# One VectorE instruction that adds the bias, scales and folds the maximum in every attention

## The reference, cut to what matters

```python
# sliding window of the first block: a mask, and a sink as one more column
s = jnp.einsum('bnqhgd,bnkhd->bnhgqk', qb, kk).astype(jnp.float32) * (D ** -0.5)
s = jnp.where(valid[None, :, None, None], s, -1e30)
p = jax.nn.softmax(jnp.concatenate([s, sink], axis=-1), axis=-1)[..., :-1]
# differential attention of the second block: a bias by distance, two softmaxes
s = jnp.einsum('bqmhd,bkmhd->bmhqk', qi, k).astype(jnp.float32) * (Dk ** -0.5) + bias
s = jnp.where(dist >= 0, s, -jnp.inf)
p = jax.nn.softmax(s, axis=-1)
w = p[:, 0] - lam * p[:, 1]
o = jnp.einsum('bhqk,bkhd->bqhd', w.astype(v.dtype), v)
# latent attention of the odd layer: a causal mask only
s = (jnp.einsum('bqhd,bkhd->bhqk', qn, k_nope) + jnp.einsum('bqhr,bkr->bhqk', qr, k_rope)) * scale
s = jnp.where((start + jnp.arange(Q_BLOCK))[:, None] >= kpos[None, :], s, -jnp.inf)
p = jax.nn.softmax(s, axis=-1).astype(v.dtype)
```

## Time and profile before

| | |
|---|---|
| three runs | 2165.37, 2166.03, 2175.59 us; median 2166.03 |
| profiled execution | span 2161.3 us from the first to the last instruction (no time of its own beside it; the median is 4.7 us above this span) |
| TensorE busy | 2005.7 us (93%), 9889 matmuls |
| VectorE busy | 1158.1 us (54%), 1710 instructions |
| ScalarE busy | 964.1 us (45%), 1758 instructions |
| mean granted TensorE clock | 0.970 |

### The profile page before, as it was taken

One profiled execution on the slowest core, in us unless ns is written; L12 is line 12 of the kernel. 1 busy time (PEld: TensorE's weight loads), 2 busy tenths in 40 slices (PEclk: granted clock), 3 DMA queues, 4 the chain that ended last, 5 costly groups with the idle time before them and its releaser, 6 DMA issues.

```text
span 2161.3 us, 25017 instructions
## 1 busy us (share of the span) xinstructions
PE 2005.7 (93%) x9889; PEld 1489.3 (69%) x9889; DVE 1158.1 (54%) x1710; ACT 964.1 (45%) x1758; POOL 12.7 (1%) x28
## 2 busy tenths in 40 slices
PE   8999889999889998779999999999888899999997
PEld 4875455776456887446788888787555578888885
DVE  6624955623965223946655543532676676555433
ACT  4735755734664332554422222344566644222223
POOL 2000000000000000000000000000000000000000
PEclk8999989999899999899999999999999999999999
DMA  8331342231212532003233333333400023333331
GB/s 296 109 86 54 142 117 59 82 86 49 79 39 68 166 98 59 1 1 112 69 98 98 98 91 98 95 100 82 132 1 1 21 88 88 98 98 98 88 100 47
DMA packets 301265, 183.11 MB, mean 85 GB/s; under 512 B 17550, under 2 KB 292108, under 8 KB 299948
## 3 DMA queue, kind: packets, MB, share of 16 engines
q1 hardware_dynamic: 295437, 166.05, 26.5%
q10 hardware_dynamic: 4704, 13.31, 1.7%
q0 software_dynamic: 1008, 2.15, 0.3%
HBM read 179.22 MB, written 2.27 MB: 84 GB/s over the span
## 4 chain that ended last, share of the span: by engine, by line
PE 78%; DVE 14%; ACT 5%; issue 2%; DMA 1%; DVEq 0%; ACTq 0%
PE PS L901 22%; PE PS L903 21%; PE PS L902 21%; PE PS L1057 2%; PE PS L1044 2%; PE PS L1072 2%; DVE SE L2145 2%; DVE TINY L2161 1%; DVE WLO L2075 1%; PE PS L1013 1%; DVE X L2042 1%; DVE S L2223 1%; ACT WHI L1510 1%; ACT SE L1638 1%; DVE SE L2192 1%
## 5 line engine op out<-in xcount | busy, mean ns | idle before, releaser
L902 PE MATMUL PS<-LO,WHI 128*128 128x512 f32 x1690 | 660.0, 391 | 0.0
L901 PE MATMUL PS<-HI,WHI 128*128 128x512 f32 x1578 | 627.0, 397 | 24.8 <-DVE LO L2048 10.0
L903 PE MATMUL PS<-HI,WLO 128*128 128x512 f32 x1578 | 616.4, 391 | 0.0
L2075 DVE TENSOR_TENSOR WLO<-RING,WHI 128x1024 fp32r<-128x1024 f32 (+3 forms) x271 | 314.5, 1161 | 530.5 <-ACT WHI L1510 529.4
L1510 ACT ACTIVATE WHI<-RING 128x1024 fp32r<-128x1024 f32 (+3 forms) x271 | 272.6, 1007 | 468.9 <-PE PS L903 446.5
L901 PEld LDWEIGHTS PS<-HI,WHI 128*128 128x128 f32 x1578 | 297.3, 188 | 107.9 <-issue 26.6
L902 PEld LDWEIGHTS PS<-LO,WHI 128*128 128x128 f32 x1690 | 318.9, 189 | 65.0 <-issue 1.7
L903 PEld LDWEIGHTS PS<-HI,WLO 128*128 128x128 f32 x1578 | 297.3, 188 | 63.4
L901 PE MATMUL PS<-HIDDEN,WHI 128*128 128x512 f32 x352 | 137.1, 390 | 0.6 <-PE PS L903 0.6
L903 PE MATMUL PS<-HIDDEN,WLO 128*128 128x512 f32 x352 | 137.0, 389 | 0.0
L902 PE MATMUL PS<-HIDDEN,WHI 128*128 128x512 f32 x352 | 136.9, 389 | 0.0
(11 more groups left out here) (342 smaller groups left out, 2361.1 us busy)
## 6 DMA issues: line engine op xcount, KB each, us to landing
RING<-in_ffn_w_up SPq DMA_DIRECT2D x88, 512.0 KB, 3.8
RING<-in_w_in SPq DMA_DIRECT2D x48, 512.0 KB, 3.8
RING<-in_w_mod SPq DMA_DIRECT2D x32, 512.0 KB, 4.4
RING<-in_ffn_w_down SPq DMA_DIRECT2D x32, 512.0 KB, 4.0
RING<-in_ev_w_in SPq DMA_DIRECT2D x30, 512.0 KB, 3.8
RING<-in_w_out SPq DMA_DIRECT2D x16, 512.0 KB, 4.3
RING<-in_od_w_in SPq DMA_DIRECT2D x15, 512.0 KB, 3.9
RING<-in_ffn_w_down SPq DMA_DIRECT2D x16, 384.0 KB, 3.4
```

The costliest lines, as they stand in the source:

```text
L901: mm(bank, WHI[i2][:, i, :], hi, start=(k == 0), stop=False)
L902: mm(bank, WHI[i2][:, i, :], lo, start=False, stop=False)
L903: return mm(bank, WLO[i2][:, i, :], hi, start=False, stop=last)
L2075: tt(WLO[i2][:, 0:nk, :], raw, WHI[i2][:, 0:nk, :], ALU.subtract).then_inc(me.signals(w_split), 1)
```

## The change

VectorE's two passes over the scores become one instruction for each head and group, `tensor_tensor_reduce`. It computes out = (score + bias) x (-scale) and folds min(first, out) over the row into one value per query, which it writes beside the output. So scores are kept negated, the minimum is the negated maximum, and ScalarE's exponential takes scale -1 instead of 1. For this the table of biases is multiplied by eight where it is evicted (the scale of these attentions is 1/8; masks are 0 or -1e30 and need nothing), and the sinks are negated once, at the start of the first mixer stage. The first value of the minimum is 3e38, in the sliding window the negated sink, and in the later groups of a joint unit the minimum of the group before, for which VectorE waits. In the sliding window the copy of the sinks goes ahead of the wait for the scores.

The semaphores `at_free` and `at_max` become one, `at_scaled`, counted once for each new instruction; `swa_free` and `swa_max` become `swa_scaled`. ScalarE waits before each exponential for the instruction that made its input. TensorE waits for both instructions of a group before it writes into the group's banks again, and in the sliding window for the one of the same bank.

```diff
                 def scores(u, g):
                     if g["free"]:
-                        pe.wait_ge(at_free, g["free"])
+                        pe.wait_ge(at_scaled, g["free"])
...
                 def scores(i):
                     u = todo[i]
-                    if n0 + i:
-                        pe.wait_ge(swa_free, n0 + i)
                     for a in range(2):
+                        if n0 + i:
+                            pe.wait_ge(swa_scaled, 2 * (n0 + i) - 1 + a)
...
                 def exp(u, i):
-                    if i == 0:
-                        act.wait_ge(at_max, u["maxima"])
+                    act.wait_ge(at_scaled, u["maxima"][i])
...
-                    fn(x, x, ACT.Exp, bias=UNIT_MAX[u["n"] % 2][:, at:at + 1], scale=1.0,
+                    fn(x, x, ACT.Exp, bias=UNIT_MAX[u["n"] % 2][:, at:at + 1], scale=-1.0,
...
                     n = todo[i]["n"] + 1
-                    act.wait_ge(swa_max, n0 + i + 1)
                     for a in range(2):
                         at = 2 * (i % 3) + a
-                        fn(pair_e(i % 3, a, n), PAIR_S[:, i % 3, a, 0:n], ACT.Exp, bias=NMAX[:, at:at + 1], scale=1.0,
+                        act.wait_ge(swa_scaled, 2 * (n0 + i) + a + 1)
+                        fn(pair_e(i % 3, a, n), PAIR_S[:, i % 3, a, 0:n], ACT.Exp, bias=NMAX[:, at:at + 1], scale=-1.0,
...
-                        fn(VECS_SB[:, c:c + w], bank[0:16, 0:w], ACT.Copy).then_inc(me.signals(acc_free_act), 1)
+                        fn(VECS_SB[:, c:c + w], bank[0:16, 0:w], ACT.Copy, scale=8.0).then_inc(me.signals(acc_free_act), 1)
...
-                    for g in u["groups"]:
+                    for n, g in enumerate(u["groups"]):
                         dve.wait_ge(at_scores, g["ready"])
-                        both = PS[:, g["bank"]:g["bank"] + 2, 0:g["n"]]
-                        if u["gates"] and g["side"]:
-                            both = PS[:, g["bank"], 0:2 * g["n"]].rearrange("p (a n) -> p a n", a=2)
-                        stt(buf[:, :, g["c"]:g["c"] + g["n"]], both, u["scale"], g["bias"],
-                            ALU.mult, ALU.add).then_inc(me.signals(at_free), 1)
-                    dve.wait_ge(*me.last)
-                    if u["joint"]:
-                        nc.vector.tensor_reduce(nmax[:, 0:2], buf, AX.X, ALU.max, negate=True).then_inc(me.signals(at_max), 1)
-                        return
...
+                        for a in range(2):
+                            at = u["softmaxes"][a if u["joint"] else 2 * n + a][3]
+                            score = PS[:, g["bank"] + a, 0:g["n"]]
+                            if u["gates"] and g["side"]:
+                                score = PS[:, g["bank"], a * g["n"]:(a + 1) * g["n"]]
+                            first = HUGE
+                            if u["joint"] and n:
+                                dve.wait_ge(at_scaled, g["count"] - 3 + a)
+                                first = nmax[:, at:at + 1]
+                            nc.vector.tensor_tensor_reduce(buf[:, a, g["c"]:g["c"] + g["n"]], score, g["bias"][:, a, :], -u["scale"],
+                                                           first, ALU.add, ALU.min, nmax[:, at:at + 1]).then_inc(at_scaled, 1)
...
-                    dve.wait_ge(swa_scores, 2 * (n0 + i + 1))
-                    stt(PAIR_S[:, r, :, 0:n], PS[:, 0:2, 0:n], 64 ** -0.5, u["bias"].unsqueeze(1).broadcast_to([P, 2, n]),
-                        ALU.mult, ALU.add).then_inc(me.signals(swa_free), 1)
                     nc.vector.tensor_copy(PAIR_S[:, r, :, n:n + 1], SINKS[:, h0:h0 + 2].unsqueeze(2)) \
                         .then_inc(me.signals(dve_step), 1)
-                    dve.wait_ge(*me.last)
-                    nc.vector.tensor_reduce(NMAX[:, 2 * r:2 * r + 2], PAIR_S[:, r, :, 0:n + 1], AX.X, ALU.max, negate=True) \
-                        .then_inc(me.signals(swa_max), 1)
+                    for a in range(2):
+                        dve.wait_ge(swa_scores, 2 * (n0 + i) + a + 1)
+                        nc.vector.tensor_tensor_reduce(PAIR_S[:, r, a, 0:n], PS[:, a, 0:n], u["bias"], -64 ** -0.5,
+                                                       SINKS[:, h0 + a:h0 + a + 1], ALU.add, ALU.min,
+                                                       NMAX[:, 2 * r + a:2 * r + a + 1]).then_inc(swa_scaled, 1)
...
+                        ts(SINKS, SINKS, -1.0, None, ALU.mult).then_inc(me.signals(dve_step), 1)
+                        dve.wait_ge(*me.last)
                     mixers(l)
```

More of the change, by code:

```diff
@@ L32 @@
 NEG = -1e30
+HUGE = 3e38
 LAYERS = 2
@@ L317, in build @@
         acc_ready, acc_free_act, acc_free_dve = sem("acc_ready"), sem("acc_free_act"), sem("acc_free_dve")
-        at_scores, at_free, at_max, at_exp, at_probs, at_turned, at_turn_free, at_values, at_mixed = (
-            sem(f"at_{n}") for n in ("scores", "free", "max", "exp", "probs", "turned", "turn_free", "values", "mixed"))
+        at_scores, at_scaled, at_exp, at_probs, at_turned, at_turn_free, at_values, at_mixed = (
+            sem(f"at_{n}") for n in ("scores", "scaled", "exp", "probs", "turned", "turn_free", "values", "mixed"))
         sq_ready, sq_used, rstd_ready, normed = sem("sq_ready"), sem("sq_used"), sem("rstd_ready"), sem("normed")
@@ L330, in build @@
         keys_to_exp, keys_exp, keys_ready = (sem(n) for n in ("keys_to_exp", "keys_exp", "keys_ready"))
-        swa_scores, swa_free, swa_max, swa_exp, swa_recip, swa_probs, swa_turned, swa_turn_free, swa_values, swa_mixed = (
-            sem(f"swa_{n}") for n in ("scores", "free", "max", "exp", "recip", "probs", "turned", "turn_free", "values", "mixed"))
+        swa_scores, swa_scaled, swa_exp, swa_recip, swa_probs, swa_turned, swa_turn_free, swa_values, swa_mixed = (
+            sem(f"swa_{n}") for n in ("scores", "scaled", "exp", "recip", "probs", "turned", "turn_free", "values", "mixed"))
         ret_scores, ret_masked, ret_values, ret_mixed = (sem(f"ret_{n}") for n in ("scores", "masked", "values", "mixed"))
@@ L667, in count_units @@
         def count_units():
-            n_unit = n_score = n_free = n_max = n_exp = n_prob = n_value = 0
+            n_unit = n_score = n_scaled = n_exp = n_prob = n_value = 0
             mains, sides = [], []
@@ L676, in count_units @@
                     g["bank"] = 4 if g["side"] else 2 * (len(mains) % 2)
-                    n_score, n_free = n_score + 2, n_free + 1
-                    g["ready"], g["count"] = n_score, n_free
-                    seen.append(n_free)
-                n_max += u["side"] + 1 if not u["joint"] else 1
+                    n_score, n_scaled = n_score + 2, n_scaled + 2
+                    g["ready"], g["count"] = n_score, n_scaled
+                    seen.append(n_scaled)
                 n_exp += len(u["softmaxes"])
@@ L683, in count_units @@
                 n_value += 2
-                u["maxima"], u["exps"], u["probs"], u["done"] = n_max, n_exp, n_prob, n_value
+                u["exps"], u["probs"], u["done"] = n_exp, n_prob, n_value
+                u["maxima"] = [n_scaled - 1 + a for a in range(2)] if u["joint"] else \
+                    [g["count"] - 1 + a for g in u["groups"] for a in range(2)]
                 u["turn"], u["ring"] = len(TURN_BANK), len(OWNER)
@@ L1076, in head_sums @@
                 def head_sums():
-                    pe.wait_ge(at_free, units[-1]["groups"][-1]["count"])
+                    pe.wait_ge(at_scaled, units[-1]["groups"][-1]["count"])
                     for k in range(4):
@@ L2147, in scaled @@
-                    dve.wait_ge(*me.last)
-                    if u["joint"]:
-                        nc.vector.tensor_reduce(nmax[:, 0:2], buf, AX.X, ALU.max, negate=True).then_inc(me.signals(at_max), 1)
-                        return
-                    c, k, m = 0, 0, u["n_main"]
-                    if u["side"]:
-                        c, k = u["groups"][0]["n"], 2
-                        nc.vector.tensor_reduce(nmax[:, 0:2], buf[:, :, 0:c], AX.X, ALU.max, negate=True) \
-                            .then_inc(me.signals(at_max), 1)
```

8 lines of the change are left out of this document (removed).

## The result

The changed kernel takes 2134.82 us (median of 4 runs, 2131.75 to 2140.63) against 2168.28 us for the kernel before, measured beside it: a ratio of 0.9855, 95% interval 0.9837 to 0.9872. The profiled execution has a span of 2131.7 us, its own time is 2133.54 us. In every profiled execution on record the time is 1.8 to 2.0 us above the span; so of the 4.7 us that the prediction carried over, some 2.8 were a profiled execution that was quicker than its median. From span to span the gain is 29.6 us.

The account below looks back on a forecast made before the run. TensorE holds 78% of the chain, but VectorE's passes hold it up in five attention stretches. Savings of 5 + 8 + 7 + 3 = 23 us take the span from 2161.3 to 2138.3; with 4.7 carried over, 2143 us, range 2132 to 2163.

Parts of the forecast that it names:

- the 4.7 us that the prediction carried over: Whole kernel: the median of the runs, 2166.03 us, lay this far above the profiled span and was added to the forecast.
- The 23 us: All attention stages: forecast gain in span, summed from 5 for mixers, 8 even, 7 gated and 3 causal.
- rival (c): New VectorE instruction everywhere: streams at half rate, 2.08 ns an element, so the kernel ends slower, 2182 us; chance 0.12.
- rival (a): New VectorE instructions, 122 on the chain: the accumulator costs its full 0.19 us, leaving 2156 us; chance 0.18.
- Mixer, 5 us: Sliding window pairs in both mixer layers: 0.38 us saved a full pair, 0.13 a half; 5.7 us on the chain, 5 kept.
- Even attention, 8 us: First part of the even attention: differential and first two joint units save 11.3 us on the chain, 8 kept.
- Gated units, 7 us: Odd attention's gated units: 1.8 us saved for 512 elements and 1.2 for 384; 8.4 us on the chain, 7 kept.
- the full 8.4: Odd attention's gated units: saving in us if every piece on the chain counts, four of 1.8 and one of 1.2.
- the lower end of the range: Whole kernel: 2132 us, from the full 29.5 us of savings and some clock that denser work gives back.
- Causal units, 3 us: Odd attention's causal units: passes save 5.2 us, but TensorE waited only 4.1 us for VectorE, so 3 kept.
- the cap of 4.1: Odd attention's causal units: TensorE waited only this many us for VectorE, so no more could be gained.
- Rival (b): Even, gated and causal stretches: TensorE becomes the bound, its waits turning to ScalarE or its own order; 2154 us; chance 0.14.

Follow-up runs that it names:

- swa_only: Changed kernel with the new instruction only in the sliding window of both mixer stages, all other attention put back to the two passes; ratio 0.9983 to the kernel before.
- even_only: Changed kernel with the new instruction only in the even attention's differential and joint units, the rest put back to the two passes; ratio 0.9962 to the kernel before.
- causal_only: Changed kernel with the new instruction only in the odd attention's causal units, the rest put back to the two passes; ratio 0.9994 to the kernel before.
- after_again: The changed kernel as it is, profiled and timed a second time; median 2136.33 us, ratio 0.9859 to the kernel before.
- gated_only: Changed kernel with the new instruction only in the odd attention's 16 gated units, the rest put back to the two passes; ratio 0.9929 to the kernel before.
- coarse_waits: Changed kernel, but ScalarE waits once a unit for all new instructions instead of before each exponential; 2140.31 us, ratio 0.9871 to the kernel before.
- after_filled: Changed kernel with unread matmuls ahead of TensorE's probability waits in joint units, differential units and both mixer stages; 2141.39 us, ratio 0.988 to the kernel before.
- the filled kernels: Kernels with unread matmuls ahead of TensorE's probability waits: the kernel before at ratios 1.0015 and 1.001, the changed one at 0.988, with an added reduction 0.9919.
- dose_three: Changed kernel with three extra VectorE reductions of 256 constant elements in each gated unit; 2152.01 us, ratio 0.9927 to the kernel before.
- dose_one_filled: Changed kernel with one extra VectorE reduction and three or one unread matmuls ahead of TensorE's probability wait in each gated unit; 2147.78 us, ratio 0.9919.

## Why the prediction was right, and where its size was off

The mechanism that was forecast is there: TensorE's waits for VectorE shrank where the chain of work had shown them. The 23 us are close to the 21.5 us by which TensorE's idle time fell, but the parts of the sum miss in both directions: the mixers gave nearly nothing and the even part's waits too little, the gated and causal units more than was kept. That they nearly cancel is luck. The other part of the gain is the clock, which the sum didn't hold.

**All gated-stage profiles together.** Old code (before, swa_only, even_only, causal_only): 107.1 to 111.0 us, idle 21.7 to 23.5, clock 0.83 to 0.89. New code (after, after_again, gated_only, coarse_waits, after_filled): 88.3 to 94.0 us, idle 14.1 to 14.7, clock 0.91 to 0.98. Neither the idle times nor the clocks overlap. The means are 108.2 and 90.5 us: 17.7 us, of which 8.1 are idle time and 9.5 are busy time. That the clock rose was therefore not chance; how far it rose in the first profile was in part. That a TensorE kept busier gets the higher clock is supported by the filled kernels, but no rule that gives the clock from the waits comes out of these runs: dose_three has less idle time than the old code and the lowest clock of all.

A second path to the clock's part uses whole times. The changed kernel's eight executions have granted clocks of 0.971 to 0.976 and times of 2142.36 down to 2131.75 us; a line through them falls by 1.8 us for each 0.001. The kernel before gives 1.9 in one set of 25 executions and 0.7 and 1.7 in two more of 13, 1.6 in all 51, with a mean clock of 0.968; the changed kernel's mean is 0.974. Of the 31 us between their means, 2136.3 and 2167.4 us (the 25), some 10 go with the clock. This is an estimate, since a line shows only that the two move together. The other 21 would be the passes, for which 23 had been forecast; the idle time of the two pages gives the same, 21.5 us.

**Prices.** 1.04 ns an element held: 686 ns a row for 512 elements (684 expected), 421 for 256 (417). The Trainium skill's half-rate rule ("Vector Engine (DVE) Microarchitecture Reference", "Points that are easy to get wrong") is for two SBUF sources; with one in PSUM the full rate was measured, so rival (c) fell. The accumulator read is a row of 83 ns, as "VectorE: DVE Perf Modes" of the Trainium skill says in kind, "Two Vector instructions with no wait between them". It was priced at 0.08 us. By the starts it costs 0.02 at most: 0.61 us an instruction, where the sum had 0.59 without it and 0.67 with it. It lay near the lower bound, and rival (a) fell. The first value from SBUF costs 59 ns (745 against 686 ns), as priced.

**Mixer, 5 us: the step that failed.** The waits of L1118 for VectorE fell from 6.1 to 3.0 us in the second mixer stage, and its length from 96.1 only to 95.7 us, in after_again to 95.65 us. The rows of L1116 before, L1118 after:

```profile
L1116 PE MATMUL PS<-Z 64*128 64x256 f32 (+1 forms) x64 | 11.5, 433 | 6.8 <-DVE S L2223 6.1 <-ACTq L1961 0.7
```
```profile
L1118 PE MATMUL PS<-Z 64*128 64x256 f32 (+1 forms) x64 | 13.9, 439 | 3.7 <-DVE TINY L2216 3.0 <-ACTq L1962 0.7
```

The same 64 matmuls hold TensorE 2.4 us longer, though one takes as long as before. This repeats: 11.1 to 11.9 us in the six profiles whose mixer has the old passes, 13.6 to 14.2 us in seven with the new instruction. I put it down to the new wait between the two scores of a pair; it wasn't tried apart from the new instruction. TensorE's wait for ScalarE's probabilities (L1125, now L1127) is 9.9 us on both sides. The two mixer stages from the first scores to the last turned block, before and then swa_only:

```profile
186.74:278.74 92.00, 75.92 (x513) 38.43 (x514) 81.21 (x130) 64.60 (x157) 0.00 (x0) 0.94 0.28 97
516.27:606.97 90.70, 71.64 (x469) 38.82 (x470) 78.63 (x129) 64.52 (x157) 0.00 (x0) 0.91 0.15 47
```
```profile
186.69:278.55 91.86, 77.75 (x513) 39.46 (x514) 74.64 (x164) 64.01 (x157) 0.00 (x0) 0.94 0.29 97
516.10:606.34 90.24, 75.28 (x470) 42.18 (x470) 71.63 (x161) 63.79 (x157) 0.00 (x0) 0.90 0.15 47
```

Idle time fell by 2.0 and 4.1 us, together a little more than the 5 us of the sum, and busy time rose by 1.8 and 3.6 us, which the sum had at nothing; 0.6 us are left of the two stages. In dose_three and dose_one_filled, where the second stage has before's clock (0.91), it takes 94.0 us, 2.1 less than before; elsewhere a little more time at the lower level takes most of that. The whole times of swa_only allow more, 3.7 us with an interval of 0.2 to 6.9, and don't contradict it.

**Even attention, 8 us.** Idle time fell by 5.2, and the clock gave 5.0 in the changed kernel (44.8 to 45.0 us at 0.96 in five profiles of that code). In even_only the stretch gained 6.6 us, 5.3 of it idle, at a clock of 0.86. Only two thirds of the waits term came: the waits for a free bank barely fell (5.9 to 5.3 us), and 1.6 us of waits for ScalarE are new. The total passed 8 us by a second cause that wasn't in the sum.

**Gated units, 7 us.** Idle time fell by 8.1 to 8.3, over the 7 kept and just under the full 8.4. That is partly luck: each unit of 512 saved 2.2 us and not 1.8, which had left more to save than came. The missing term is the clock: some 9.5 us. I had it only as a remark on the lower end of the range ("some clock that denser work gives back"), and the earlier trace rows with 0.84 and 0.90 there, beside 1.00 in the causal stretch, had shown that there was something to win.

**Causal units, 3 us.** 4.0 us, the cap of 4.1 and not the value kept. Nothing held it back.

**What would show it.** The waits for L2188 and L2192 were to fall under 4 us: 3.1 and 2.2 us. Rival (b) came only in small part: the turned blocks' waits for ScalarE's L1648 are 1.6 us in the even stretch, where there were none before, and 0.7 in the gated one, as before. In the gated unit shown, no new instruction held the queue before it started.

## What to carry to other kernels

Where a stage's granted clock is below 1.00 and its engine waits, price the passes by the idle time that they can give back, and then add the clock as a term of its own: here it was an estimated 10 of some 31 us. Cut both traces at the same matmuls and split each stage into busy and idle time before explaining anything: in the gated stage idle time repeated within 2 us from profile to profile of the same code, busy time only within 6. Look also at what the new waits do to TensorE's busy time: in the mixers they ate what the shorter waits had given. For parts of a few microseconds read the stretch, since the whole time moves by more than that with the clock.

## What the runs showed of the hardware

- At the same program, TensorE's busy time in one stage was 74.2 and 79.9 us, at granted clocks of 0.98 and 0.91.
- Little VectorE work can go with much by the clock: in one profile each, 5.3 us of it came with a stage 5.9 to 11.6 us longer, 15.7 us with one 16.7 to 22.4 us longer.
- Matmuls that nobody reads, put into TensorE's waits, raised the gated stage's granted clock from 0.87 to 0.93 and 0.97, and the whole kernel was no faster (ratios 1.0015 and 1.001).
- The row that reads the accumulator out on VectorE (83 ns) starts with its follower and delays it by 0.02 us at most; ScalarE's did by 0.10 us.
